# A two-block transformer layer: the two-operand work of GpSimd and the attention masks on VectorE

## What is computed

```python
h = rmsnorm(x); proj = h @ w_in; gates = sigmoid(proj[..., 6144:] + b_gate)
y_a = gelu(u) * (tril(W_s) @ rmsnorm(gelu(v)) + b)
bb  = k * b;  s[t] = ab * s[t-1] + bb @ u[t]               # complex state, 64 groups of 64
y_b = glu(gelu(re(c * s) + d * u))
y_c = stick_breaking_attention(q, k, v)                     # w = exp(log_sigmoid(z) + after), s < t only
x = x + (gates[0]*(y_a@w0) + gates[1]*(y_b@w1) + gates[2]*(y_c@w2)) @ w_out
x = rmsnorm(x + square(relu(rmsnorm(x) @ w_mlp_in)) @ w_mlp_out)
# second block
ua = za[:768] * sigmoid(za[768:]);  va = silu(layernorm(conv31(ua)))
yc = gb * conv3(gc * xv);           yb = (pooled means) @ w_grp * scale
x = x + (g_a*(va@w_a) + g_b*(yb@w_b) + g_c*(yc@w_c)) @ w_o
out = rmsnorm(x + square(relu(rmsnorm(x) @ w_up)) @ w_down)
```

## Time and profile before

| | |
|---|---|
| three runs | 2962.98, 2964.06, 2964.64 us, median 2964.06 |
| the profiled execution | 2963.64 us; its span 2961.7 us |
| busy, share of the span | TensorE matmuls 99%, weight loads 81%, VectorE 58%, ScalarE 46%, GpSimd 2% |
| mean granted TensorE clock | 0.996 of full speed |
| DMA | 561 MB, 189 GB/s over the span |

### The profile page before, as it was taken

One profiled execution on the slowest core, in us unless ns is written; L12 is line 12 of the kernel. 1 busy time (PEld: TensorE's weight loads), 2 busy tenths in 40 slices (PEclk: granted clock), 3 DMA queues, 4 the chain that ended last, 5 costly groups with the idle time before them and its releaser, 6 DMA issues.

```text
span 2961.7 us, 33940 instructions
## 1 busy us (share of the span) xinstructions
PE 2918.7 (99%) x13892; PEld 2403.7 (81%) x13892; DVE 1730.3 (58%) x1835; ACT 1367.7 (46%) x1570; POOL 60.3 (2%) x34
## 2 busy tenths in 40 slices
PE   8999999999999999999999999999999999999998
PEld 6788878888878888888888787888887888888886
DVE  6588854456655455554556678866655555455554
ACT  5544444554445444444445444444445444444443
POOL 1100000011000000000000000000000000000000
PEclk9999999999999999999999999999999999999999
DMA  8566755555655656555556656666555555656554
GB/s 281 165 195 196 203 167 184 179 160 188 209 174 185 198 174 203 185 181 188 195 179 228 182 170 192 198 192 210 179 201 180 190 185 183 197 175 203 186 179 155
DMA packets 290746, 561.01 MB, mean 189 GB/s; under 512 B 17696, under 2 KB 24608, under 8 KB 289952
## 3 DMA queue, kind: packets, MB, share of 16 engines
q1 hardware_dynamic: 290592, 558.85, 58.9%
HBM read 556.68 MB, written 2.10 MB: 189 GB/s over the span
## 4 chain that ended last, share of the span: by engine, by line
PE 77%; issue 18%; DVE 3%; POOL 1%; ACT 1%; DMA 0%; DVEq 0%; SPq 0%; ACTq 0%; POOLq 0%
PE ACC L569 75%; PE TB L525 2%; DVE WL L1232 1%; DVE CA L1667 1%; POOL QKV L1810 0%; ACT WH L820 0%; DMA RAW<-in_w_in_dram 0%; DVE X L1630 0%; DVE WGC L1715 0%; DVE X L1588 0%; PE TB L771 0%; ACT JK L838 0%; DMA SS<-in_x_t_dram 0%; POOL SS L1797 0%; POOL SS L1794 0%
## 5 line engine op out<-in xcount | busy, mean ns | idle before, releaser
L1232 DVE TENSOR_TENSOR WL<-RAW,WH 128x1024 fp32r<-128x1024 f32 (+1 forms) x1024 | 1252.7, 1239 | 883.1 <-ACT WH L820 881.5
L820 ACT ACTIVATE WH<-RAW 128x1024 fp32r<-128x1024 f32 (+1 forms) x1024 | 1063.3, 1054 | 973.3 <-PE ACC L569 913.5
L569 PE MATMUL ACC<-WH,XTH 128*128 128x512 f32 (+1 forms) x2720 | 1071.9, 394 | 30.3 <-DVE WL L1232 24.8
L569 PE MATMUL ACC<-WH,XTL 128*128 128x512 f32 (+1 forms) x2720 | 1060.1, 390 | 0.0
L569 PE MATMUL ACC<-WL,XTH 128*128 128x512 f32 (+1 forms) x2720 | 1058.7, 389 | 0.0
L569 PEld LDWEIGHTS ACC<-WH,XTH 128*128 128x128 f32 x2720 | 513.1, 189 | 139.5 <-DVE WL L1232 19.7
L569 PEld LDWEIGHTS ACC<-WH,XTL 128*128 128x128 f32 x2720 | 512.7, 189 | 107.4
L569 PEld LDWEIGHTS ACC<-WL,XTH 128*128 128x128 f32 x2720 | 513.5, 189 | 102.4
L569 PE MATMUL ACC<-WH,YAH 128*128 128x512 f32 x864 | 338.6, 392 | 0.0
L569 PE MATMUL ACC<-WH,YAL 128*128 128x512 f32 x864 | 336.5, 389 | 0.0
L569 PE MATMUL ACC<-WL,YAH 128*128 128x512 f32 x864 | 336.1, 389 | 0.0
(11 more groups left out here) (247 smaller groups left out, 1066.9 us busy)
## 6 DMA issues: line engine op xcount, KB each, us to landing
RAW<-in_w_in_dram SPq DMA_DIRECT2D x256, 512.0 KB, 4.3
RAW<-in_w_mlp_in_dram SPq DMA_DIRECT2D x128, 512.0 KB, 3.9
RAW<-in_w_mlp_out_dram SPq DMA_DIRECT2D x128, 512.0 KB, 4.5
RAW<-in_w_up_dram SPq DMA_DIRECT2D x128, 512.0 KB, 3.9
RAW<-in_w_down_dram SPq DMA_DIRECT2D x128, 512.0 KB, 4.6
RAW<-in_w_gate_dram SPq DMA_DIRECT2D x96, 512.0 KB, 4.0
RAW<-in_w_branch_dram SPq DMA_DIRECT2D x48, 512.0 KB, 4.4
RAW<-in_w_out_dram SPq DMA_DIRECT2D x32, 512.0 KB, 4.6
```

What stands on the lines that cost most here:

```text
L569: ins = e.matmul(ACC[:, 2 * (b % 2) + half, 0:n], p[:, k, xs], q[:, t, 0:n], start=(k == 0 and m == 0), stop=(k == nk - 1 and m == 2))
L820: e.activation(WH[u % NSPL][:, :, 0:n], RAW[u % NRAW][:, :, 0:n], ACT.Copy).then_inc(hi, 1)
L1232: e.tensor_tensor(l, r, h, ALU.subtract).then_inc(lo, 1)
```

## The change

- The four products of c and k are no longer made side by side in SS. A new task `s5_out` on VectorE makes CT in place and then CAK, with two temporaries in TMP: 12 operations, one a unit, in units 23 to 28 and 29 to 34. `ab` moves from units 23, 24 to 22, 23, `k0` from 33 to 36, and the scan starts at unit 35 with 0.79 steps a unit. ScalarE's `s5_bu` no longer waits for CAK.
- The masks become two VectorE operations of 128x1024 in each half: a product with a 0/1 constant and a minimum with a constant of 3e38 and -1e30. The constants CST grow from 3 to 5 columns of 128.
- The adds of `bc` and `b2c` move into `branch_next` on VectorE, right behind their products.
- The products of za, zc and branch c move to VectorE: za's as a fourth step at unit 560, zc's behind the last zc eviction, branch c's at unit 620.
- GpSimd keeps the tril select (now first in its queue) and the two memsets.

Cut to its core (waits that only change their count are left out):

```diff
-    at("s5_mat", 14, 9)
-    at("ab", 23, 2)
-    at("s5_mat", 24)
+    at("s5_mat", 14, 8)
+    at("ab", 22, 2)
+    at("s5_out", 23, 6)
...
-    at("k0", 33)
-    at("scan", 31, 71, 0.76)
+    at("s5_out", 29, 6)
+    at("k0", 36)
+    at("scan", 35, 71, 0.79)
...
+    at(("ev", "za"), 560)
...
+    at("cc", 620)
...
+            e.tensor_tensor(t0, CTV[0], kim, ALU.mult).then_inc(c_done, 1)
+            yield
+            e.tensor_tensor(t1, CTV[1], kim, ALU.mult).then_inc(c_done, 1)
+            yield
+            e.wait_ge(c_done, 1)
+            e.tensor_tensor(CTV[0], CTV[0], kre, ALU.mult).then_inc(c_done, 1)
+            yield
...
+            e.wait_ge(at_m, hg + 1)
+            for buf, keep, op in ((SPb, AFTER, ALU.mult), (ZSb, BOUND, ALU.min)):
+                v = buf.rearrange("p (h b c) -> p h b c", h=4, b=3)[:, :, 0:3:2, :]
+                e.tensor_tensor(v, v, keep.unsqueeze(1).unsqueeze(1).to_broadcast([P, 4, 2, P]), op).then_inc(at_k, 1)
+            yield
...
+                evicted(e, br, c)
+                if merged % 8:
+                    e.wait_ge(mgv, merged - 4 + c + 1)
+                e.tensor_tensor(M[:, :, cs], M[:, :, cs], SGx[:, :, cs], ALU.add).then_inc(mgv, 1)
...
+        def za_product():
+            e.wait_ge(za_sig, 1)
+            e.tensor_tensor(ZA[:, :, 0:768], ZA[:, :, 0:768], ZA[:, :, 768:1536], ALU.mult).then_inc(ua_prod, 1)
+            yield
+
+        def zc_out():
+            for _ in range(4):
+                yield
+            for c in range(1, 5):
+                evicted(e, "zc", c)
+            e.tensor_tensor(ZC[:, :, 768:1536], ZC[:, :, 768:1536], ZC[:, :, 1536:2304], ALU.mult).then_inc(zc_prod, 1)
+            yield
+
+        def conv_c_out():
+            e.wait_ge(cc_tap, 18)
+            emptied(e, "gbt", 2)
+            emptied(e, "gbt", 1)
+            e.tensor_tensor(GBT[:, :, :], GBT[:, :, :], WGC[:, :, :], ALU.mult).then_inc(vc_done, 1)
+            yield
```

More of the change, by code:

```diff
@@ L33, in consts @@
     c[:, 2 * P:3 * P] = 1.0
+    c[:, 3 * P:4 * P] = i[None, :] > i[:, None]
+    c[:, 4 * P:5 * P] = np.where(i[None, :] > i[:, None], 3e38, -1e30)
     s, t = np.arange(L)[:, None], np.arange(L)[None, :]
@@ L145, in build @@
     par_v, par_a = sem("s5_par_vector"), sem("s5_par_scalar")
[L146 to L147 removed]
+    gx_done, powers, c_done, ws_done = sem("gain_x2"), sem("s5_powers"), sem("s5_c"), sem("gm_tril")
+    ca_done, ab_done = sem("s5_ca"), sem("s5_ab")
     scan, ug_done = sem("s5_scan"), sem("s5_gelu")
[L149 removed]
+    vn_done, sig, mgv = sem("gm_v_norm"), sem("gate_sigmoid"), sem("merged")
     glu_sig = sem("glu_sigmoid")
@@ L1386, in s5_mat, with s5_out @@
             e.tensor_tensor(z[2], z[2], z[3], ALU.add).then_inc(ab_done, 1)
-            e.wait_ge(ck, 4)
-            e.tensor_tensor(CTV[0], CZ[0], CZ[1], ALU.subtract).then_inc(c_done, 1)
             yield
-            e.scalar_tensor_tensor(out=CTV[1], in0=CZ[2], scalar=-1.0, in1=CZ[3], op0=ALU.mult, op1=ALU.subtract).then_inc(c_done, 1)
-            yield
-            e.wait_ge(ak, 4)
-            e.tensor_tensor(CAV[0], CZ[0], CZ[1], ALU.add).then_inc(ca_done, 1)
-            e.tensor_tensor(CAV[1], CZ[3], CZ[2], ALU.subtract).then_inc(ca_done, 1)
+        def s5_out():
+            t0, t1 = (TMP[:, z, :, :].rearrange("p a (j c) -> p (a j) c", c=32) for z in range(2))
+            kre, kim = (PR[:, 19 + k, :].unsqueeze(2).to_broadcast([P, 32, 32]) for k in range(2))
+            wr, wi = (A1[:, k, :].unsqueeze(2).to_broadcast([P, 32, 32]) for k in range(2))
+            e.wait_ge(ld["s5c"], 32)
+            e.wait_ge(powers, 24)
+            e.tensor_tensor(t0, CTV[0], kim, ALU.mult).then_inc(c_done, 1)
+            yield
+            e.tensor_tensor(t1, CTV[1], kim, ALU.mult).then_inc(c_done, 1)
[3 more added lines that the diff above has]
+            yield
+            e.wait_ge(c_done, 3)
+            e.tensor_tensor(CTV[0], CTV[0], t1, ALU.subtract).then_inc(c_done, 1)
+            yield
+            e.wait_ge(c_done, 2)
+            e.tensor_tensor(CTV[1], CTV[1], kre, ALU.mult).then_inc(c_done, 1)
+            yield
+            e.wait_ge(c_done, 5)
+            e.scalar_tensor_tensor(out=CTV[1], in0=CTV[1], scalar=-1.0, in1=t0, op0=ALU.mult, op1=ALU.subtract).then_inc(c_done, 1)
+            yield
+            e.wait_ge(c_done, 6)
+            e.tensor_tensor(t1, CTV[1], wi, ALU.mult).then_inc(ca_done, 1)
+            yield
+            e.tensor_tensor(CAV[0], CTV[0], wr, ALU.mult).then_inc(ca_done, 1)
+            yield
+            e.wait_ge(ca_done, 2)
+            e.tensor_tensor(CAV[0], CAV[0], t1, ALU.add).then_inc(ca_done, 1)
+            yield
+            e.tensor_tensor(t0, CTV[0], wi, ALU.mult).then_inc(ca_done, 1)
+            yield
+            e.tensor_tensor(CAV[1], CTV[1], wr, ALU.mult).then_inc(ca_done, 1)
+            yield
+            e.wait_ge(ca_done, 5)
+            e.tensor_tensor(CAV[1], CAV[1], t0, ALU.subtract).then_inc(ca_done, 1)
@@ L1556, in branch_first, with branch_next @@
                 yield
-        def branch_next(br, g, SGx, M=None, pooled=0, before_=0):
+        def branch_next(br, g, SGx, M, merged):
             for c in range(4):
@@ L1652, in za_out @@
                 yield
+            yield from za_product()
+        def za_product():
+            e.wait_ge(za_sig, 1)
+            e.tensor_tensor(ZA[:, :, 0:768], ZA[:, :, 0:768], ZA[:, :, 768:1536], ALU.mult).then_inc(ua_prod, 1)
+            yield
+        def zc_out():
+            for _ in range(4):
+                yield
+            for c in range(1, 5):
+                evicted(e, "zc", c)
+            e.tensor_tensor(ZC[:, :, 768:1536], ZC[:, :, 768:1536], ZC[:, :, 1536:2304], ALU.mult).then_inc(zc_prod, 1)
+            yield
+        def conv_c_out():
[3 more added lines that the diff above has]
+            e.tensor_tensor(GBT[:, :, :], GBT[:, :, :], WGC[:, :, :], ALU.mult).then_inc(vc_done, 1)
+            yield
         def taps():
@@ L1729, in pool_groups @@
                 yield
-        tasks = {"x_split": x_split, "x_norm": x_norm, "s5_par": s5_par, "s5_mat": s5_mat, "scan": s5_scan, "v_norm": v_norm,
+        tasks = {"x_split": x_split, "x_norm": x_norm, "s5_par": s5_par, "s5_mat": s5_mat, "s5_out": s5_out, "scan": s5_scan, "v_norm": v_norm,
                  "gm0": lambda: gm(0), "gm1": lambda: gm(1), "gt": lambda: place("gt", UT, 8), ("ev", "glu"): glu_out,
@@ L1778, in stream, with gm_tril @@
             front()
[L1780 to L1797, removed]
+        def gm_tril():
             e.wait_ge(ld["gw"], 32)
@@ L1801, in s5_mat @@
             yield
[L1803 to L1819, removed]
         def pad():
@@ L1825, in pad @@
             yield
[L1827 to L1851, removed]
+        tasks = {"gm_tril": gm_tril, "block1_end": pad}
         run(e, stream, tasks)
```

48 lines of the change are left out of this document (22 added, 26 removed).

## The result

The changed kernel took 2944.98 us (median of 6 runs, 2943.96 to 2946.07) where the kernel before took 2964.35 on the same chip (6 runs, 2959.11 to 2965.51): a ratio of 0.9937 with a 95% interval of 0.9925 to 0.995, so 19.4 us faster. Forecast were 2947 and a gain of 17.0. The profiled execution took 2944.32 us, its span 2942.5, its mean granted clock 0.998.

The account below looks back on a forecast made before the run. TensorE, busy 99%, was taken to bound the kernel by its own work and its waits. Gains less costs summed to 17.0 us, from 2963.64 to 2946.6, plus 0.42 for the median: 2947; range 2943 to 2956.

Parts of the forecast that it names:

- the long VectorE instructions are not GpSimd's doing: Rival: only the two direct waits, 2.4 and 1.2 us, go, less 1.2 of costs: 2961.6 us; chance 0.06.
- First batch: Four state-space products, units 18 and 19: wait of 3.82 us and slow stretch of 2.45 go, together 6.3.
- second batch: State-space products, units 26 and 27: TensorE's wait of 2.38 us at 98.06 goes, gain 2.4.
- masks of the second half: At unit 204: TensorE's wait of 1.17 us for GpSimd's four selects goes, gain 1.2.
- za: Product of za, unit 561: TensorE's wait of 2.23 us at 1651.51 goes, gain 2.2.
- branch c: Last product of branch c, unit 621: TensorE's wait of 2.16 us goes, gain 2.2 with nothing to spare.
- Product of zc: Units 599 to 602: wait of 1.92 us and 1.6 of slow clock go, 0.4 of wait stays, gain 3.1.
- Small waits at units 35 and 36: As the K0 matmuls move, two VectorE cuts come about 1 us late each, cost 0.7 more than now.
- The masks' price: A 128x1024 VectorE mask operation: taken as 1.22 us, at most 2.6, which would cost 2.8 in the first half.
- The adds: Eight adds of the merged branches, moved to VectorE: nothing gained or lost; without cover, 9.1 us.
- The early room: Rival: VectorE has no room in the first 36 units, 9.1 us reach TensorE, gain 8.8: 2955 us; chance 0.14.
- VectorE the bound: Rival: all 27.8 us of work handed to VectorE show, making 2973 us, slower; chance 0.06.

Follow-up runs that it names:

- 1 to 3: Changed kernel plus an unused 128x1536 GpSimd operation at each of the three former product places, reading two, one or no operands: 2952.4, 2955.06, 2945.9 us.
- experiment 6: Changed kernel with the K0 matmuls back at unit 33 instead of 36: 2944.23 us.
- 4: Changed kernel with the eight adds of the merged branches back on GpSimd: 2944.38 us.
- experiment 11: Changed kernel with each of the three second-block products preceded by a VectorE maximum of the same size: 2951.32 us in one run.

## Why the prediction was right

*What bounds the kernel.* Right: the gain is that of TensorE's waits, and 58% of a mean busy share said nothing against giving VectorE 27.8 us more work. VectorE's total fell, since it had been charged for the time in which it was held.

*The cause of the waits.* Right as to the mechanism: put back alone, GpSimd's operation brings the held instruction, the wait and the slow clock back (1 to 3). That rules out the rival that the long VectorE instructions are not GpSimd's doing. Its condition was drawn too narrowly, as shown there, and its words "the same picture comes back" at each wait were too wide: at 98.06 and 634.65 VectorE and TensorE waited for GpSimd's results, and at 634.65 the operations were selects with one operand, beside which cuts were held already in the kernel before.

*The terms that go.* First batch, second batch, masks of the second half, za and branch c came within 0.15 us of the forecast. Product of zc: 3.5 against 3.1; of the 0.4 that was to stay as a wait, none stands at 602, and the 0.78 at 1735.10 comes ahead of the product. That closeness is in part luck, since it is measured against the one profile from which the forecast was read. Against the second profile of the kernel before the same places give 5.0, 5.1, 1.5, 2.4 and 4.0, and zc 1.55: the waits recur, the slow clock behind them moves. The waits were read by walking VectorE's queue with three durations: 1.14 for a cut, 0.8 for two taps, 1.67 for a product.

*The terms that stay.* Small waits at units 35 and 36, cost 0.7: shown, and by experiment 6 it is the move of K0. The masks' price was the open one, and the lower bound held: the group of mask operations has a mean of 1216 ns.

```profile
L1546 DVE TENSOR_TENSOR QKV<-QKV,CST 128x1024 f32<-128x1024 f32 x4 | 4.7, 1216 | 0.0
```

The mask wait itself was given as near 0.3 and is 0.56: the cost of 0.3 comes on top of the 0.25 that stood there.

*The adds.* Nothing, as forecast (4).

*The early room.* That rival fell: the net cost of units 22 to 36 is 1.0, not 9.1.

*VectorE the bound.* It fell in the whole, but experiment 11 shows that it holds locally: at units 562, 601 and 622 one product more passes on 1.4 to 2.2 us. Had VectorE needed twice as long for a product, the three places would have lost 7 of the 8.3 us that they gained.

*The size.* The sum was 17.0, the places forecast gave 17.6 against the first profile of the kernel before and 18.2 against the second, the medians 19.4 (19.7 on another chip). The sum took the slow stretches that one profile showed, 2.45 and 1.6, and the second profile has another set. Between the two spans unit 768 makes 1.4 of the difference and the start 0.3, and both vary between executions of one kernel. What the remaining 1.2 to 1.8 us between the places and the medians are is not shown; it would take the unit times of many executions. Nor is it known whether unit 768 is at low clock less often after the change: it is in both profiles of the kernel before (4.64, 4.80), in one of the two of the changed kernel, and in seven of the ten of its variants.

## What to carry to other kernels

Where a VectorE instruction lasts as long as a GpSimd operation beside it, count GpSimd's work at VectorE's price as well: moved over, a product of 128x1536 cost 1.67 us and gave back a hold of 2.4 to 3.3 us (a cut of 3.67 where one takes 1.22, a tap of 3.73 where one takes 0.48). Look for it only where the held engine is next on the bounding engine's path; eight adds, each with a hold of about 2 us, were worth nothing. And forecast from unit-by-unit times and a walk of the queue, not from busy shares, keeping the slow-clock stretches of one profile apart as a term that another execution may not have.

## What the runs showed of the hardware that was not expected

- A GpSimd operation with one SBUF operand (a tensor_scalar) took longer than a product that names the same tile twice (4.09 against 2.75 us for 128x1536, both beside VectorE) and held VectorE at least as long (3.40 against 2.93). A memset of that size took 1.39 and held nothing.
- The hold works in the other direction too. Of the four equal selects of the second half in the kernel before, the first three took about 1.6 us each beside cuts, the first two of them 3.13 together, and the last 0.63 alone:

```profile
629.30 3.13 POOL L1810 TENSOR_SCALAR_AFFINE_SELECT QKV<-QKV 128x512 f32<-128x512 f32 x2 [30.68 <-DVE QKV L1506]
...
633.96 0.63 POOL L1810 TENSOR_SCALAR_AFFINE_SELECT QKV<-QKV 128x512 f32<-128x512 f32 x1
```

- The low clock behind a wait is a matter of the execution. The same kernel had it at units 18, 19 and 602 in one profile and at 18, 19, 26, 27 and 622 in another. Behind the last projection's transposes unit 768 took 4.5 to 4.8 us in ten of fourteen profiles and 3.2 to 3.3 in the others, though TensorE's idle time before it was 2.71 us in all of them.
